# Sample outputs through the DMA transpose, scores before masked keys, and more work held back at the ends of a retention layer

## The reference, cut to what matters

```python
q, k, v = rotate(h @ w_q), rotate(h @ w_k) / 16, h @ w_v          # per head
scores = (q @ k.T) * intra                                        # chunks of 128 rows, decay mask
o = scores @ v + (q @ s) * q_decay                                # s is the state, 256 x 512
s = s * chunk_decay + (k * k_decay).T @ v
o = (o - mean(o)) * rsqrt(var(o) + eps)                           # group norm over the 512 of a head
y = (silu(h @ w_g) * o) @ w_o
```

## Time and profile before

| | |
|---|---|
| median of 3 runs (lowest, highest) | 2001.91 us (1998.64, 2004.72) |
| the profiled execution: its own time | 1995.12 us |
| its span on the slowest core, core 7 | 1994.1 us |
| spans of the eight cores | 1970.7 to 1994.1 us |
| TensorE (PE) busy on core 7 | 1861.9 us, 93% |
| VectorE (DVE), ScalarE (ACT), GpSimd (POOL) busy | 44%, 34%, 11% |
| mean granted TensorE clock, core 7 | 0.980 |

### The profile page before, as it was taken

One profiled execution on the slowest core, in us unless ns is written; L12 is line 12 of the kernel. 1 busy time (PEld: TensorE's weight loads), 2 busy tenths in 40 slices (PEclk: granted clock), 3 DMA queues, 4 the chain that ended last, 5 costly groups with the idle time before them and its releaser, 6 DMA issues.

```text
span 1994.1 us, 29657 instructions; the slowest of 8 cores (1970.7 to 1994.1 us)
## 1 busy us (share of the span) xinstructions
PE 1861.9 (93%) x10183; PEld 857.4 (43%) x10183; DVE 875.6 (44%) x1549; ACT 679.8 (34%) x1066; POOL 222.2 (11%) x363
## 2 busy tenths in 40 slices
PE   4999989999999999999879999999999889899997
PEld 1444444344444333343334444545454533455553
DVE  3565533434356663434555554332223556422225
ACT  3544433322224742123344443221022366210112
POOL 0111111010111010101001111101011010011010
PEclk9999999999999999999989999999999999899999
DMA  9434556797996259998636665755345240254352
GB/s 194 73 64 80 93 77 109 197 203 174 208 200 134 43 101 218 204 208 205 141 110 118 104 93 82 128 71 73 53 65 80 44 64 1 33 82 72 51 73 95
DMA packets 214257, 220.27 MB, mean 110 GB/s; under 512 B 45632, under 2 KB 168896, under 8 KB 214080
## 3 DMA queue, kind: packets, MB, share of 16 engines
q0 software_dynamic: 128112, 114.08, 40.2%
q1 hardware_dynamic: 86000, 104.30, 17.7%
HBM read 277.10 MB, written 48.89 MB: 163 GB/s over the span
## 4 chain that ended last, share of the span: by engine, by line
PE 79%; DVE 7%; DMA 6%; issue 4%; ACT 3%; POOL 0%; DVEq 0%; SPq 0%; ACTq 0%; POOLq 0%
PE ps L579 79%; DVE rt L603 2%; DMA wr<-w 1%; DMA x_62<-xTp 1%; DMA uT_64<-g_73 1%; DMA S_2_109<-st_in 1%; DMA wr<-wa 1%; DVE stat L858 1%; DMA x_63<-xTp 1%; PE ps L584 0%; DVE h_44 L606 0%; ACT sq L595 0%; DVE x_62 L606 0%; DVE h_45 L606 0%; DMA yTp<-x_62 0%
## 5 line engine op out<-in xcount | busy, mean ns | idle before, releaser
L579 PE MATMUL ps<-h_44,wr 128*128 128x512 bf16 x1824 | 416.2, 384 | 14.0 <-DMA wr<-wa 8.4
L579 PE MATMUL ps<-h_45,wr 128*128 128x512 bf16 x1824 | 415.3, 381 | 1.2 <-ACT s_104 L595 1.2
L579 PEld LDWEIGHTS ps<-h_44,wr 128*128 128x128 bf16 x1824 | 175.8, 99 | 231.7 <-issue 35.3
L579 PEld LDWEIGHTS ps<-h_45,wr 128*128 128x128 bf16 x1824 | 174.2, 98 | 219.3 <-issue 21.9
L259 POOL DMA_DIRECT2D wr<-w x152 | 112.9, 746 | 1012.3 <-PE ps L579 904.1
L579 PE MATMUL ps<-aT_103,wr 128*128 128x512 bf16 x704 | 159.0, 381 | 1.2 <-DVE aT_136 L603 1.1
L595 ACT ACTIVATE s_104<-ps 128x512 f32<-128x512 f32 x88 | 52.4, 596 | 310.9 <-PE ps L579 283.5
L579 PE MATMUL ps<-aT_105,wr 128*128 128x512 bf16 x704 | 157.6, 379 | 0.0
L603 DVE TENSOR_TENSOR aT_103<-s_104,ps 128x512 bf16<-128x512 f32 x88 | 60.4, 688 | 216.7 <-PE ps L579 195.9
L603 DVE TENSOR_TENSOR aT_105<-s_106,ps 128x512 bf16<-128x512 f32 x88 | 60.5, 688 | 210.2 <-PE ps L579 181.5
L579 PE MATMUL ps<-wr,h_44 128*128 128x512 bf16 (+1 forms) x576 | 130.0, 374 | 6.0 <-ACT rstd_57 L595 3.6
(11 more groups left out here) (294 smaller groups left out, 2152.7 us busy)
## 6 DMA issues: line engine op xcount, KB each, us to landing
wr<-w POOLq DMA_DIRECT2D x88, 512.0 KB, 7.1
wr<-wa POOLq DMA_DIRECT2D x24, 1024.0 KB, 11.6
wr<-w POOLq DMA_DIRECT2D x64, 352.0 KB, 7.0
wr<-wo POOLq DMA_DIRECT2D x16, 512.0 KB, 8.4
S_0_107<-st_in SPq DMA_DIRECT2D x16, 512.0 KB, 6.2
S_1_108<-st_in SPq DMA_DIRECT2D x16, 512.0 KB, 6.9
S_2_109<-st_in SPq DMA_DIRECT2D x16, 512.0 KB, 6.3
S_3_110<-st_in SPq DMA_DIRECT2D x16, 512.0 KB, 6.6
```

Of the source, the lines that this page charges most:

```text
L579: self.S.op("pe", lambda e: e.matmul(out, lhsT, rhs, start=start, stop=stop, skip_group_check=skip), r, w, dur=k * max(0.1, self.n(out) * ...
```

## The change

Four edits.

1. `fin2` is gone. `fin` creates `uTs` and gives `gn_gate` a `post` step, a DMA transpose of `us` into `uTs` on the SP queue. The four TensorE transposes and the ACT copy of each of the four heads go.
2. In `head`, the scores and their mask (`sTs`) are emitted before `KZ` and `Qz`.
3. `late` is the last five pieces of `P(3, 1)` instead of three; the last merge of a layer has five output blocks instead of six, and three run after it.
4. Bookkeeping: `r_o(n)` may be picked only when the value and gate units of its chunk have been emitted.

```diff
         def need_o(n):
...
-            return self.need([sTb[n % 2], v[p][1][c]] + Sbf[n % 2][1], [bank[6]])
+            nd = self.need([sTb[n % 2], v[p][1][c]] + Sbf[n % 2][1], [bank[6]])
+            return lambda: nd() if have_vg(n) else 1e9
...
-                        main, late = main[:-3], main[-3:]
+                        main, late = main[:-LATE], main[-LATE:]
...
-                    main = late + wo_p(0, range(6))
+                    main = late + wo_p(0, range(5))
...
-        X.run(wo_p(0, (6, 7)))
+        X.run(wo_p(0, (5, 6, 7)))
...
+            bk, bb = self.pb(UB)
+            for a in range(2):
+                self.mm(bk[:, :128], k_[:, a, :], q_[:, a, :], a == 0, a == 1, kb + qb, [bb])
+            sT_, sTb_ = self.SS["sT"]
+            self.tt(sT_[:, :], bk[:, :128], cb[:, CB_MNEW:CB_MNEW + 128], ALU.mult, [bb, cbb], sTb_)
             for j in range(4):
                 self.ts(KZ[:, j, :], kt_[:, :], cf[:, CF_JM + j:CF_JM + j + 1], ALU.mult, ktb + [cfb], KZb)
...
-            for ec in range(4):
-                self.tr(bv[:, ec * 128:(ec + 1) * 128], u_[:, ec * 128:(ec + 1) * 128], ub_, [bb])
-            t, tb = self.M.tile(f"uTs{h}", [128, 4, NS], BF16, self.rid0 + h * 3584)
-            self.uTs[h] = (t, tb)
-            self.act(t[:, :, :], bv[:, 0:512].rearrange("p (a b) -> p a b", a=4), AF.Copy, [bb], tb)
+            t, tb = self.uTs[h] = self.M.tile(f"uTs{h}", [128, 4, NS], BF16, self.rid0 + h * 3584)
+
+            def post():
+                self.dma_tr(t[:, :, :], u_[:, :], ub_, tb, "uts")
+            self.SS["gn"] = self.gn_gate(ps[:, 4, :], self.bank[4], cf[:, e:e + 1], g_[:, :], gb_[0], on_[:, :], onb_[0], u_[:, :], ub_[0], post)
```

More of the change, by code:

```diff
@@ L975, in fn @@
                         self.act(g[p][0][:, c, :], bk, AF.Silu, [bb], [g[p][1][c]])
+                    have.add((kind, h, ti, c))
                     if last and c == 3 and scx is None:
@@ L1060, in ret_layer @@
         gnj = [None, None]
+        have = set()
         def par(h, ti):
@@ L1074, in r_o @@
         def r_o(n):
+            assert have_vg(n)
             h, ti, c = seq[n]
@@ L1132, in need_sc, with have_vg @@
             return self.need(k[p][1] + q[p][1], [bank[7]])
+        def have_vg(n):
+            return all((kind,) + seq[n] in have for kind in "vg")
         def need_o(n):
@@ L1201, in ret_layer @@
         late = []
+        LATE = 5
         for h in range(RH):
@@ L1260, in head @@
                         cb[:, CB_QM:CB_QM + 512].rearrange("p (j t) -> p j t", j=4), ALU.mult, qb + [cbb], Qzb)
[L1261 to L1265, removed]
         def head2(h):
@@ L1312, in fin @@
             e = CF_ECS + h
[L1313 to L1319, removed]
-            for ec in range(4):
-                self.tr(bv[:, ec * 128:(ec + 1) * 128], u_[:, ec * 128:(ec + 1) * 128], ub_, [bb])
-            t, tb = self.M.tile(f"uTs{h}", [128, 4, NS], BF16, self.rid0 + h * 3584)
-            self.uTs[h] = (t, tb)
-            self.act(t[:, :, :], bv[:, 0:512].rearrange("p (a b) -> p a b", a=4), AF.Copy, [bb], tb)
+            if "gn" in self.SS:
+                self.force(self.SS["gn"])
+            t, tb = self.uTs[h] = self.M.tile(f"uTs{h}", [128, 4, NS], BF16, self.rid0 + h * 3584)
+            def post():
+                self.dma_tr(t[:, :, :], u_[:, :], ub_, tb, "uts")
+            self.SS["gn"] = self.gn_gate(ps[:, 4, :], self.bank[4], cf[:, e:e + 1], g_[:, :], gb_[0], on_[:, :], onb_[0], u_[:, :], ub_[0], post)
         SS, bank, R = self.SS, self.bank, self.R
@@ L1351, in ret_sample @@
                 out.append((1, lambda h=h: fin(h), None))
-                out.append((1, lambda h=h: fin2(h), self.need(SS["u"][1], pool=UB)))
         if x_free:
```

## The result

The changed kernel takes 1977.41 us, median of four runs (1974.14 to 1981.69); the kernel before beside it 2000.28 us (1993.46 to 2004.72). The ratio is 0.989, interval 0.9855 to 0.9925. The forecast was 1985.5 us, within 1974 to 1999.

The account below looks back on a forecast made before the run. TensorE, busy 93% of core 7's span, plus its standstills was taken as the bound, on cores 7 and 3. Terms 9.3 + 2.7 + 3.5 + 2.9 - 2.0 = 16.4 us off 2001.9 gave 1985.5 us, range 1974 to 1999.

Parts of the forecast that it names:

- Sample outputs: Sample outputs by DMA transpose: TensorE's waits for `us`, sixteen transposes and some clock loss go; 9.3 us saved, bounds 0 to 9.3.
- the clock, which I had counted behind the longest wait alone: Sample outputs: eleven matmuls behind the 4.11 us gap return to full clock, 3.85 to 2.54 us; 1.3 us saved.
- The transposes' price on SP: Sample outputs' DMA transposes on the SP queue: taken as nothing because 18.3 us of SP time lie free.
- Scores: Sample scores ahead of `KZ` and `Qz`: 2.5 us at heads 1 to 3, 0.2 at head 0; 2.7 us, bounds 0 to 4.6.
- The ends: Work held back at both retention layers' ends: 3.5 us first, 2.9 second, less 2.0 for new waits; 4.4 us saved.
- the 1.38 us: Second retention layer's end: output of chunk 27 starts at 1208.97 instead of 1210.35, part of the 2.9 us there.
- that 1.37 us: First retention layer's end: output of chunk 27 starts at 262.37 instead of 263.74, part of the 3.5 us there.
- the new waits: Both ends: chunk 29's output follows close on its scores and state copy; 0.98 us each, 2.0 us lost.
- the clock behind the block: First output block at each end: half the lower-clock loss goes, 1.4 us at the first end, 0.8 at the second.
- the ends stay as they are: Rival: w_o loads set the transposes' landing, earlier issue does nothing, each end gives 0.7 us; 1990.5 us, chance 0.19.
- State traffic: Rival: feed-forward state loads do not speed up and take the gain, only the ends count; 1997.5 us, chance 0.17.
- the SP queue: Rival: transposes of heads 0 and 2 hold up state loads on SP, TensorE stops at query matmuls; 2012.8 us, chance 0.07.

Follow-up runs that it names:

- edit 1 alone: Kernel before with only the sample outputs moved to DMA transposes, scores and ends unchanged: 0.9933 of before, mean span -12.0 us.
- edit 3 alone: Kernel before with only the last value and gate pieces and three output blocks held back at both retention ends: 0.9987 of before, mean span -1.3 us.
- before with the semaphores: Kernel before with only head 3's output transposes put on eight DMA semaphores of their own: 0.9974 of before, mean span -5.2 us.
- edit 2 alone: Kernel before with only the sample scores put ahead of masked keys and queries: 0.9981 of before, mean span -3.4 us.
- the three of the changed kernel: Three measurements of the same changed kernel, all edits in: 0.989, 0.9887 and 0.9884 of before.
- the later gate: Changed kernel with the sample gate put 12 us later into the engines' orders: 0.9893 of before, mean span 1967.7 us.
- the third run of the changed kernel: Changed kernel measured once more, nothing altered: 0.9884 of before, mean span 1966.5 us.
- with the w_o loads out of the way: Changed kernel with the w_o loads for the last query, key and value slots held until chunk 27's transpose has landed: 1.002 of before.
- the later loads: Changed kernel with the w_o loads for the last query, key and value slots issued only once chunk 27's transpose is issued: 0.9896 of before.
- second run of the changed kernel: Changed kernel measured again beside the single-edit kernels, nothing altered: 0.9887 of before, mean span 1967.9 us.

## Why the prediction was right, and where it was not

**Sample outputs, 9.3 us predicted, 12.0 measured** (edit 1 alone, error about 2). The row taken for the wait was typical: `us` cost 2.8 to 9.7 us on the eight cores of the profile before, 6.7 in the mean, against 6.9 on core 7. Most of the other 2.7 us is the clock, which I had counted behind the longest wait alone. From the end of the first retention layer to the first scores of the second, the granted clock cost TensorE (each stretch's time, times the share of full speed that was missing) 13.4 us, as a mean over the cores of three profiles with edits 1 and 2 absent (before, edit 3 alone, before with the semaphores), and 10.0 us with edit 1 alone: 3.4 us instead of 1.3. In the same stretch 7.5 us of standing still went instead of 6.9, and 7.5 + 3.4 + 1.1 make the 12.0. The transposes' price on SP was nothing, as chosen.

**Scores, 2.7 predicted, 3.4 measured.** The mechanism held row by row: 3.0 us of `sTs` went on core 7, and 1.6 us stayed at head 0, where VectorE's norm outputs hold it.

**The ends, 3.5 + 2.9 - 2.0 = 4.4 predicted, 1.3 measured.** This is the step that failed, most of all at the second end. A stretch that all these kernels share, from the scores of chunk 20 to the last output block of the layer, tells the ends apart (means of the eight cores). At the first end it took 125.9 to 127.0 us in the three profiles with the ends as they were (before, edit 1 alone, edit 2 alone), and 124.3 to 125.5 us in five with edit 3 (alone, the three of the changed kernel, the later gate): 1.6 us less. At the second it took 127.2 to 130.0 and 128.3 to 129.6 us: nothing. Predicted were 3.5 - 1.0 = 2.5 and 2.9 - 1.0 = 1.9 us.

The term that was wrong is the 1.38 us by which the output of chunk 27 was to start earlier at the second end. TensorE had waited there for the keys of a transpose, in a row that the earlier trace rows leave out; with the change it waits for that chunk's own scores. Core 7, before and then with the change:

```profile
1210.15 0.22 PE L584 MATMUL ps<-cbt,k_68 128*128 128x128 bf16 x1 [0.85 <-DVE k_68 L603]
```

```profile
1196.23 0.38 PE L579 MATMUL ps<-v_71,sT 128*128 128x512 bf16 x1 [1.11 <-DVE sT L603]
```

So 0.85 us went and 1.11 came, and the same two numbers stand on every core of every profile looked at. At the first end the 0.98 us of the earlier trace rows did go; what is left of that 1.37 us is a score piece and a key transpose that now run at another place, which is no gain. With chunk 29's 0.79 and 0.55 us the new waits come to 2.5 us instead of 2.0. And of the clock behind the block, 0.4 us went at the first end (mean of the same profiles) instead of 1.4, and none at the second instead of 0.8.

The wait for chunk 27's transpose did get shorter, and the table of waits does not show it, since it puts part of that wait under other names. Core 2, before: the block's wait, then the transpose that it was waiting for:

```profile
277.94 5.23 PE L579 MATMUL ps<-uT_64,wr 128*128 128x512 bf16 x16 [2.11 <-ACT rkt_99 L595]
...
L625 SPq DMA_TRANSPOSE uT_64<-g_73 x1: 1254/1254/1254, 268.6 to 268.6; - x1
...
DMA to landing us min/median/max: 9.1/9.1/9.1
```

The transpose lands at 277.7, and the block starts 0.24 us later. It starts 0.24 us after that landing at both ends on all eight cores of this profile, whatever name the table gives; on core 0 it starts before the copy `rkt_99` has begun (270.26 and 270.87 us). By the gaps themselves the eight cores waited 3.7 us at the two ends in the profile before, not the 2.3 us that the table's `uT_64` lines make, and 5.7 and 6.6 us in those of edits 1 and 2 alone; with edit 3 it is 2.9 to 4.2 us in the five profiles. So core 7's 6.0 us were not far from the kernel's mean, and the own semaphores took away what was there: 3.7 us of waits and 1.8 us of clock behind them before, 5.2 us measured.

The rival "the ends stay as they are" had the cause of the long landing right: 10.9 us before, 10.3 in the third run of the changed kernel, 2.4 with the w_o loads out of the way. That an earlier issue does nothing is not shown. With edit 3 the transpose leaves 5.9 us behind the first of these loads at the first end (7.1 before) and lands after 9.8 to 10.5 us (9.3 to 10.7 before; means of a profile's cores). That rival's terms for the ends, 0.7 + 0.7 - 2.0, come nearer to the 1.3 than mine, though its total (1990.5 us) is farther off. The rule that it drew on, from the Trainium skill, "DMA: Bandwidth & Descriptors", section on queues, rings and completion order (an increment lands only after every earlier write of that DMA engine, across its queues), agrees with 10.3 against 2.4 us, and with the later loads, where the transpose landed 0 to 0.9 us after the last load issued ahead of it; whether the data or only the increment was late, these runs do not divide.

And there was something at the ends that I did not see, though the earlier trace rows show it: all sixteen matmuls stood behind the wait, while twelve did not need what it waited for. Its 5.2 us were there to take without any of edit 3.

**State traffic and the SP queue.** Neither rival came: no wait of TensorE for `S0f` over 0.2 us appeared, and SP stood idle behind the transpose. The free time was shorter than I said, 5.1 us instead of 18.3 (477.71 to 482.84), and still enough, since the transpose held the queue for 1.48 us and not until its landing.

**The sum and the time.** Terms 16.4 us, mean span 16 to 19 us less. That they meet is partly luck: outputs and scores gave 3.4 us more than I said, and the ends 3.1 us less. The forecast is 8.1 us too high: 1.6 us since the kernel before stood at 2000.3 and not at 2001.9 beside it, the rest mostly because one core's sum was carried over to the slowest core. Cores 7 and 3 are not the slow ones, as I had read the earlier trace rows: in the 21 runs of before each of the eight was the slowest at least twice. In the runs compared the slowest core stood 10.7 us over the mean of the eight before, and 5.4 to 7.6 us after, so the time gained 3 to 5 us more than the mean did. The likely reason is that the waits that went differed from core to core, and the core that drew the long ones set the time; no run isolates that, and edit 1 alone still has 9.7 us. The new wait behind head 1 was not predicted: I counted what the transposes put on SP, and not that the gate's two steps moved behind a load on GpSimd.

## What to carry to other kernels

Look at a wait on all cores before sizing it: where it differs between them, its mean goes into the sum, and its spread into the slowest core. Take its length from the gap before the instruction, and check the name that the table gives against the landing. When an order moves an instruction forward, ask what it will wait for at its new place. Before moving work to cover a wait, ask whether the instruction that waits needs what it waits for: a shared DMA semaphore makes the first reader wait for the last transfer. And look at what was issued ahead of a transfer: here it set the landing, 10.3 us with the w_o loads and 2.4 us without.

## What the runs showed of the hardware

The same transpose lands after 10.9 or 10.3 us with w_o loads issued ahead of it, and after 2.4 us without; with some of the loads ahead and some behind, it lands 0 to 0.9 us after the last of those ahead (above). And the clock behind a wait does not follow the wait's length alone. First output block on core 1, second run of the changed kernel, then first:

```profile
276.19 5.30 PE L579 MATMUL ps<-uT,wr 128*128 128x512 bf16 x16 [1.35 <-DMA uT<-g]
```

```profile
276.96 3.61 PE L579 MATMUL ps<-uT_64,wr 128*128 128x512 bf16 x16 [1.76 <-DMA uT_64<-g_73]
```

Sixteen matmuls lost 1.7 us behind the shorter wait and nothing behind the longer one. So the clock's share of a wait is known only from its own row, and an estimate for one not yet seen has to span both.
